# The odd mixer of a two-part block: decay as one exponential, resident gate weights, gates two projections later, 1/rms in PSUM

## The reference, cut to what matters

```python
def odd_mixer(h, w_in, conv_w, conv_b, w_rg, b_rg, w_ig, b_ig, lam, w_out):
    p = jnp.einsum("btd,dn->btn", h, w_in)
    xr, gate = jnp.split(p, [W_LRU], axis=-1)          # 1536 = 12 heads x 128 each
    xc = causal_depthwise_conv(xr, conv_w, conv_b)     # 4 taps
    xh = xc.reshape(bsz, t, LRU_HEADS, LRU_HD)
    r = sigmoid(einsum("bthi,hij->bthj", xh, w_rg) + b_rg)
    i = sigmoid(einsum("bthi,hij->bthj", xh, w_ig) + b_ig)
    log_a = -LRU_C * r * softplus(-lam)                # LRU_C = 8
    a = exp(log_a)
    mult = sqrt(-expm1(2.0 * log_a))
    bterm = mult * (i * xc)
    _, hs = associative_scan(_lin_combine, (a, bterm), axis=1)   # h = a h + b
    y = hs * silu(gate)
    return einsum("btn,nd->btd", y, w_out)
```

## Time and profile before

| | |
|---|---|
| median of 3 runs | 1165.42 us (1164.32 to 1165.55) |
| profiled execution | 1167.06 us, its span 1165.3 us |
| mean granted TensorE clock | 0.962 |
| TensorE matmul busy | 1078.4 us (93%) |
| VectorE busy | 758.8 us (65%) |
| ScalarE busy | 597.2 us (51%) |
| GpSimd busy | 600.3 us (52%) |

### The profile page before, as it was taken

The page is one execution under the profiler, slowest core; times in us unless marked ns, Lnnn a source line. Parts: engine busy times, 40 slices in busy tenths (PEclk is TensorE's granted clock), DMA queues, the critical chain, the costliest instruction groups (busy, mean ns, idle before and its releaser), DMA issues. The chain is left out here.

```text
span 1165.3 us, 21433 instructions
## 1 busy us (share of the span) xinstructions
PE 1078.4 (93%) x8189; PEld 1006.8 (86%) x8189; DVE 758.8 (65%) x1506; ACT 597.2 (51%) x1188; POOL 600.3 (52%) x453
## 2 busy tenths in 40 slices
PE   8899999999999989999999999989997879866886
PEld 8699978988889979999999999989887779655886
DVE  8859586666553245864855533369999795675964
ACT  4345667666664467644455543443334354656442
POOL 3546344445544477555344443386775654542661
PEclk9989999999999989999999999999999888888998
DMA  8224333333234423245455555544443324333342
GB/s 304 92 91 145 112 107 105 113 128 109 91 110 145 145 76 107 91 156 185 162 181 185 182 182 179 168 161 165 162 150 124 125 91 143 112 102 108 120 142 73
DMA packets 43445, 158.08 MB, mean 136 GB/s; under 512 B 4944, under 2 KB 4944, under 8 KB 43088
## 3 DMA queue, kind: packets, MB, share of 16 engines
q1 hardware_dynamic: 43200, 156.69, 39.8%
q10 hardware_dynamic: 144, 0.03, 0.0%
HBM read 155.65 MB, written 1.05 MB: 134 GB/s over the span
## 5 line engine op out<-in xcount | busy, mean ns | idle before, releaser
L1731 PE MATMUL p_proj<-arena_r,ring_hi 128*128 128x256 f32 x2208 | 661.5, 300 | 28.8 <-POOL ring_lo L548 11.1
L1732 PE MATMUL p_proj<-arena_r,ring_hi 128*128 128x256 f32 x2208 | 630.9, 286 | 0.0
L1733 PE MATMUL p_proj<-arena_r,ring_lo 128*128 128x256 f32 x2208 | 630.3, 285 | 0.0
L548 POOL TENSOR_TENSOR ring_lo<-ring,ring_hi 128x1024 fp32r<-128x1024 f32 x182 | 438.3, 2410 | 349.4 <-ACT ring_hi L877 348.5
L1731 PEld LDWEIGHTS p_proj<-arena_r,ring_hi 128*128 128x128 f32 x2208 | 429.1, 194 | 48.4 <-issue 28.3
L1732 PEld LDWEIGHTS p_proj<-arena_r,ring_hi 128*128 128x128 f32 x2208 | 430.0, 195 | 7.9 <-issue 6.0
L1733 PEld LDWEIGHTS p_proj<-arena_r,ring_lo 128*128 128x128 f32 x2208 | 429.5, 195 | 0.0
L877 ACT ACTIVATE ring_hi<-ring 128x1024 fp32r<-128x1024 f32 x276 | 290.4, 1053 | 118.8 <-PE p_proj L1733 117.8
L548 DVE TENSOR_TENSOR ring_lo<-ring,ring_hi 128x1024 fp32r<-128x1024 f32 x94 | 119.6, 1272 | 67.4 <-ACT ring_hi L877 65.9
L653 POOL TENSOR_TENSOR sbuf_s<-sbuf_s,srow 128x256 f32<-128x256 f32 (+1 forms) x48 | 41.8, 870 | 83.1 <-DVE srow L1301 58.5
L1720 PE MATMUL p_proj<-arena,ring 128*128 128x256 f32 x208 | 59.3, 436 | 24.9 <-issue 12.0
(11 more groups left out here) (274 smaller groups left out, 1243.0 us busy)
## 6 DMA issues: line engine op xcount, KB each, us to landing
ring<-w_stream SPq DMA_DIRECT2D x289, 512.0 KB, 3.3
arena<-w_tok SPq DMA_DIRECT2D x1, 1632.0 KB, 13.4
arena<-x_t SPq DMA_DIRECT2D x4, 256.0 KB, 4.9
arena<-w_cmp SPq DMA_DIRECT2D x1, 1024.0 KB, 15.3
out_t<-arena SPq DMA_DIRECT2D x4, 256.0 KB, 2.4
par<-cols SPq DMA_DIRECT2D x1, 323.0 KB, 3.0
row<-rows ACTq DMA_DIRECT2D x1, 32.0 KB, 3.2
```

The lines of the kernel that those rows point to most:

```text
L548: return eng.tensor_tensor(ring_lo[:, u % RING, :, :].rearrange("p k n -> p (k n)"), ring[:, u % RING, :, :].rearrange("p k n -> p (k n)") ...
L1731: pe.matmul(slot(s)[:, 0:S], w_hi, hi, start=(c == 0), stop=False)
L1732: pe.matmul(slot(s)[:, 0:S], w_hi, lo, start=False, stop=False)
L1733: mm = pe.matmul(slot(s)[:, 0:S], w_lo, hi, start=False, stop=(c == n - 1))
```

## The change: what it does

- xr: the conv's first part leaves ScalarE. VectorE multiplies by 1/rms, applies tap four and bias (one tensor_scalar), and adds the three taps; the banks of xr have VectorE as their only reader.
- The gates' weights (1.5 MB) are no longer in the ring. One DMA brings them into 12 free arena tiles, issued by SyncE just before the unit of even_ya[5], behind a wait for the layernorm's outputs.
- The gates of head h become one step `rgi`, two matmuls into one bank of the group `score` after xr[h+2] (heads 10 and 11: after gate[0] and gate[2]). ScalarE makes both tanh in place, U2 as before but from PSUM, and a = exp(c' r + c') into LA. The step U2 + 1 goes.
- `lru` goes: no reciprocal, no 2x - 1, no product. `lw` is two instructions: (i + 1) XC in PSUM, then (a + 1) times that into W1. `scan` multiplies W1 by U2, both in SBUF, into PSUM. The factor of `scanout` is 0.25.
- Square roots: nine heads after xr[11] (ahead of rgi of head 9), three after gate[5], each time with the table loads around them.
- scan, scanout and the split of the result run 2, 3 and 4 projections after their gate, and no longer all splits at the end.
- The copy `rin` of 1/rms in the free half of the `p_mean` bank: `hf`, `mgr` and lnv read it from there. ynorm, lnv and the last norm write it directly; for the other norms one tensor_scalar copies it at the first `hf`.

```diff
-    xr, rg_ig = jobs["xr"], jobs["rg_ig"]
     for j in range(12):
-        out.append(xr[j])
+        out.append(jobs["xr"][j])
         if j == 0:
             out += [("nsum", 3, 7), ("norm", 3)]
-        elif j not in (6, 10):
-            out.append(("scale", xr[j - 1]))
...
+        else:
+            out.append(("oconv", j - 1))
         if 2 <= j < 10:
             out += [("hf", 3, j - 2), ("split", "h3", j - 2)]
...
+        if j == 11:
+            out += [("uroot", h) for h in range(9)]
+        if j >= 2:
+            out.append(("rgi", j - 2))
+        if j >= 3:
+            out.append(("lw", j - 3))
+    gate = jobs["gate"]
     for j in range(12):
-        out.append(jobs["gate"][j])
+        out.append(gate[j])
         if j == 0:
-            out += [("uroot", h) for h in range(12)]
...
+            out += [("oconv", 11), ("lw", 9), ("gact", gate[0]), ("rgi", 10)]
+        elif j == 1:
+            out += [("lw", 10), ("gact", gate[1])]
+        else:
+            if j == 2:
+                out += [("rgi", 11)]
+            out += [("scan", j - 2), ("gact", gate[j])]
+            if j == 2:
+                out += [("lw", 11)]
+            if j == 5:
+                out += [("uroot", h) for h in range(9, 12)]
+            if j >= 3:
+                out.append(("scanout", j - 3))
+            if j >= 4:
+                out.append(("split", "ly", j - 4))
...
+                if u == first["job", "even_ya", 5] // 8:
+                    sp_eng.wait_ge(sem("yaf_ready"), 8)
+                    sp_eng.dma_start(flat(WG, 12), w_rgi).then_inc(sem("wrgi_in"), 16)
...
+                elif k == "rgi":
+                    h = s[1]
+                    ps = take(s)
+                    rg, ig = ps[:, 0:S], ps[:, S:2 * S]
+                    act.activation(rg, rg, ACT.Tanh, bias=half[:, 16 + h:17 + h], scale=0.5)
+                    act.activation(ig, ig, ACT.Tanh, bias=half[:, 28 + h:29 + h], scale=0.5)\
+                        .then_inc(sem("rgi_tanh"), 1); note(sem("rgi_tanh"))
+                    settle()
+                    act.activation(A(U2 + h), rg, ACT.Tanh, bias=half[:, 40 + h:41 + h],
+                                   scale=half[:, 40 + h:41 + h]).then_inc(sem("u_ready"), 1); note(sem("u_ready"))
+                    act.activation(A(LA + h), rg, ACT.Exp, bias=half[:, 160 + h:161 + h],
+                                   scale=half[:, 160 + h:161 + h]).then_inc(read["score", "A"], 1); note(read["score", "A"])
...
                     _, q, c = s
+                    if c == 0 and q < 4:
+                        link(dve.tensor_scalar(rin, rinv[:, :], 1.0, None, ALU.mult))
...
-                                             in1=rinv[:, :], op0=ALU.mult, op1=ALU.mult)\
+                                             in1=rin, op0=ALU.mult, op1=ALU.mult)\
...
-                        dve.tensor_tensor(A(AC + c), A(AC + c), rinv[:, :], ALU.mult).then_inc(sem("ln_z"), 1); note(sem("ln_z"))
+                        dve.tensor_tensor(A(AC + c), A(AC + c), rin, ALU.mult).then_inc(sem("ln_z"), 1); note(sem("ln_z"))
...
-                elif k == "lru":
-
-                    h = s[1]
-                    dve.wait_ge(sem("la_ready"), h + 1)
-                    link(dve.reciprocal(lru_sum(h), A(LA + h)))
-                    link(dve.tensor_scalar(A(LA + h), lru_sum(h), 2.0, -1.0, ALU.mult, ALU.add))
-                    link(dve.tensor_tensor(lru_sum(h), lru_sum(h), A(W1 + h), ALU.mult))
...
+                    was_read(dve, ("rgi", h))
+                    ig = slot(("rgi", h))[:, S:2 * S]
+                    link(dve.scalar_tensor_tensor(out=ig, in0=ig, scalar=1.0, in1=A(XC + h), op0=ALU.add, op1=ALU.mult))
+                    dve.scalar_tensor_tensor(out=A(W1 + h), in0=A(LA + h), scalar=1.0, in1=ig,
+                                             op0=ALU.add, op1=ALU.mult).then_inc(read["score", "D"], 1); note(read["score", "D"])
...
-                    link(dve.tensor_tensor(lru_sum(h), lru_sum(h), A(U2 + h), ALU.mult))
+                    link(dve.tensor_tensor(lru_sum(h), A(W1 + h), A(U2 + h), ALU.mult))
...
+                elif k == "rgi":
+                    h = s[1]
+                    readers_done(pe, s)
+                    pe.wait_ge(sem("wrgi_in"), 16)
+                    was_read(pe, ("job", "xr", h), "D")
+                    for m in range(2):
+                        mm = pe.matmul(slot(s)[:, S * m:S * m + S], wrgi[:, h, m, :], A(XC + h), start=True, stop=True)
+                    mm.then_inc(filled["score"], 1)
```

More of the change, by code:

```diff
@@ L51 @@
           ("a_gate", 8, 8), ("pool", 8, 2), ("even_yb", 8, 8), ("even_ya", 8, 8), ("xr", 12, 8), ("gate", 12, 8),
[L52 to L59, removed]
+          ("odd_out", 8, 12)]
+ON_VECTOR = {"br_dsa", "br_nsa", "br_ssd", "w_out", "ff1", "ff2", "even_yb", "even_ya", "xr", "odd_out"}
+TWICE = {"xbc", "sz", "a_gate", "b_gate", "gate"}
+LATE_TAG = {"iq": "h0u", "ik": "h0u", "dk": "h0u", "kc": "h0u", "vc": "h0u", "ks": "h0u", "kw": "h0u", "val_glu": "h2u"}
 HEAD = [("job", "iq", 0), ("job", "iq", 1), ("job", "ik", 0), ("job", "dk", 0), ("job", "kc", 0), ("job", "vc", 0),
         ("job", "ks", 0), ("job", "kw", 0)]
-LATE = HEAD + [("job", "val_glu", j) for j in range(6)] + [("job", "xr", j) for j in range(12)]
+LATE = HEAD + [("job", "val_glu", j) for j in range(6)]
 GAIN = {"h0u": "norm1", "y": "ssd_g", "h1": "norm2", "h2u": "even_g", "h3u": "odd_g"}
@@ L284, in schedule @@
+    out += [("scan", 10), ("scanout", 9), ("split", "ly", 8), ("scan", 11), ("scanout", 10), ("split", "ly", 9),
+            ("scanout", 11), ("split", "ly", 10), ("split", "ly", 11)]
     squared(4, jobs["odd_out"])
@@ L342, in psum_tenants, with program @@
     return where, turns
-def program(nc, x_t, w_stream, w_tok, w_cmp, cols, rows, out):
+def program(nc, x_t, w_stream, w_tok, w_cmp, w_rgi, cols, rows, out):
     steps = schedule()
@@ L431, in program @@
         dec = sb("dec", [P, 32])
[L432 removed]
+        half = sb("half", [P, 172])
         m8 = sb("m8", [P, 8])
@@ L479, in lru_sum @@
         def lru_sum(h):
-            at = (bank["score"] + bank["turn"] + bank["pv"])[h // 2 % 4]
+            at = (bank["turn"] + bank["pv"] + bank["score"])[h // 2 % 4]
             return at[:, S * (h % 2):S * (h % 2) + S]
@@ L749, in _ @@
             for s in steps:
-                if s in LATE:
+                if s in LATE or s[0] == "job" and s[1] == "gate":
                     continue
-                if s[0] == "scale":
+                if s[0] in ("scale", "gact"):
                     s = s[1]
@@ L1160, in _ @@
                     link(dve.tensor_scalar(half[:, 40:52], sp[:, 5, 64:76], 2.0, None, ALU.mult))
+                    link(dve.tensor_scalar(half[:, 160:172], sp[:, 5, 64:76], -4.0, None, ALU.mult))
                     dve.wait_ge(sem("ea_ready"), 1)
@@ L1450, in _ @@
                         .then_inc(sem("ybf_ready"), 1); note(sem("ybf_ready"))
-                elif k == "job" and s[1] in ON_VECTOR and s[1] != "ff1":
+                elif k == "job" and s[1] in ON_VECTOR and s[1] not in ("ff1", "xr"):
                     _, name, j = s
```

88 lines of the change are left out of this document (29 added, 59 removed).

## The result

The kernel after takes 1131.26 us in the median (1130.31 to 1133.29, 4 runs) against 1164.97 beside it: ratio 0.971, 95% interval 0.9685 to 0.9739. Forecast were 1124 and a range of 1113 to 1138. 33.7 us came instead of 41.1. The profiled execution took 1133.29 us (span 1131.5, mean clock 0.968).

The account below looks back on a forecast made before the run. Bound: TensorE's waits and low clock in the odd mixer, 50 us, from VectorE's queue. 50.0 - (3.8 + 1.4 + 0.8 + 3.4) = 40.6; less 3.0 clock, plus 3.0 and 0.5, 41.1; 1165.42 - 41.1 = 1124.3 us, range 1113 to 1138.

Parts of the forecast that it names:

- The bound: Odd mixer, square to square: 135.3 us, of which 85.3 TensorE's work and 50 waits and low clock from VectorE's queue.
- Part 1: xr turns without reciprocals: VectorE 3.9 us, TensorE 3.73; cost beyond TensorE's work 0, bounds 0 and 9 us.
- part 7: 1/rms in PSUM: 3.0 us from the layernorm's multiplications, 0.5 from hf of the even mixer and the start.
- Part 2: Gates as rgi, two projections later: 12.6 us of waits go, and the middle window's low clock with them.
- Part 3: Square roots of nine heads, then three: TensorE stalls of 3.8 us (bounds 0 and 6) and 1.4 us.
- Parts 4 and 5: Gate turns: 0.8 us lost to GpSimd, scan lock 0; end after gate[11]: 3.4 us, bounds 1 and 6.
- The clock: Remaining falls of TensorE's clock, behind the 3.8 and 3.4 us stalls: 1.4 to 2.7 us, 3.0 taken for both.
- Part 6: Gate weights in one DMA: landing 7 us after issue, cost 0; at 133 GB/s some 2 us of stall.
- The rival with the lock: Gate turns: scans wait for GpSimd, 16 us less gained, 1140; half of it, 1132. Chance 0.20, at 1134.
- The one in which all is hidden: Odd mixer: almost all waits hidden and the clock never falls, 1114 us. Chance 0.12.
- ScalarE's chain: xr turns: ScalarE's chain closes the turn, 9 us less gained, 1133. Chance 0.10.
- The rival of slower times by table loads at each head: Exp and tanh share no table, each rgi loads twice: 64 us lost against 41, about 1188. Chance 0.02.

Follow-up runs that it names:

- e6_after_recip: The kernel after with the decay by reciprocal, plain product and 2x - 1 again, its order and PSUM places kept: 1149.0 us.
- e2_rinv_sbuf: The kernel after with 1/rms back in SBUF everywhere and the copy dropped: 1146.2 us.
- e4_no_tables: The kernel after with Tanh in place of Sqrt in the root's instruction, so no change of function table in the odd mixer: 1124.0 us.
- e9_all: The kernel after with roots placed in PSUM, rgi(9) behind gate[0] and every scan one turn earlier: 1122.4 us.
- e1_scan_psum: The kernel after with the scan's product taking W1 and 1/rms in PSUM instead of W1 and the root in SBUF: 1127.6 us.
- e7_psum_root: The kernel after with the roots written or copied to PSUM by ScalarE for the scan's product, nothing left out: 1128.4 us.
- e5_before_exp: The kernel before with the decay by Exp alone, in place of reciprocal, 2x - 1 and product; old order kept: 1157.9 us.
- e11_roots84: The kernel after with PSUM roots, rgi(9) and scans moved, an early one-column tanh, and roots as eight, one xr turn earlier, then four: 1125.0 us.
- e12_scan_early: The kernel after with every scan one turn earlier and nothing else moved: 1129.3 us.
- e8_order: The kernel after with rgi(9) behind gate[0] instead of ahead of it, and every scan one turn earlier: 1125.8 us.

## Why the prediction held, and where it was short

- **The bound** (85.3 of work, 50 of waits and low clock, caused by VectorE's queue): right. e6_after_recip is the proof for the reciprocals: 2.0 us back on VectorE a head, and 15 of 30 us are gone.
- **Part 1**, xr turns at 3.9 on VectorE and 3.74 on TensorE: right to 0.01 us: VectorE's instructions repeat at 3.91 and TensorE's at 3.74. That is in part luck: oconv's tensor_scalar took 0.54 for the 0.46 put down, and the three taps 0.49 each, pipelined, for 0.51. Exp takes 0.56, between the two rows that bounded it, and no load stands between it and the tanh. But 3.9 holds only with part 7: I wrote hf at 0.51 there and sized part 7 without it. e2_rinv_sbuf shows that it is worth 10 us more there.
- **Part 2**: right; the waits of the earlier trace rows on oconv and tanh(r) are gone. Not foreseen: the table load at the first tanh and 0.6 of small pieces, 1.9 us in all.
- **Part 3**: 3.72 where I said 3.8, and 0.82 + 0.15 where I said 1.4. Right.
- **Parts 4 and 5**, the mis-sized terms. I took the lock as 0, since the scan's mean of 1.0 fitted GpSimd's 3.2, with 0.8 for the turns and 3.4 for the end. The turns did settle at 3.25, of which the lock's hold on GpSimd's split is 0.18. And VectorE had begun them late: the tanh of gate[2] stands behind rgi(11) on ScalarE, VectorE got to it at 1049.45, 3.4 us after gate[2]'s last matmul, and at 3.25 a turn against TensorE's 2.87 it never made that up. (Its 4.8 us of idle time just before are no measure of the lag: in e4_no_tables they are 2.4, and the gaps at odd_out 4.5.) What was late came due at odd_out, in gaps of 1.15, 1.70, 1.03 and 0.93 us, 4.8 in all. From 1061.85 to the square, 31.3 us hold 20.5 of work (four gates, two odd_out, one square) and 5.8 of gaps; of the 5.0 left, 1.9 stand in e9_all too, at clock 1.00: a slower pace between the gaps, whose cause is not shown. So 6.7 at the end for the 4.2 forecast. Freeing the product takes 3.6 off, in e1_scan_psum and e7_psum_root.
- **The clock**, 3.0 for both falls: it was 3.0 behind gate[2] alone (21.10 us for work of 6 x 2.87 + 0.86 = 18.1) and the other 3.1 of those 5.0 in odd_out, where the last window has 0.77. The price of one fall was right: each covered 5.5 us of work at 1.2 GHz, 25 matmuls, within the 15 to 30 and near the upper end of the 1.4 to 2.7 us read from the old chain. The step that failed is the sum: two falls make 2.8 to 5.4, and I booked 3.0.
- **Part 6**: landed 8.2 us after its issue (forecast 7); no gap at even_ya[5].
- **Part 7**: the layernorm's multiplications save 5.9 on VectorE. What of it reaches TensorE can be read from its waits between 940 and 965 us, before (first two lines) and after:

```profile
PE p_proj L1731 <- POOL arena_r L556: 3.6, 5, 1.5
PE p_proj L1731 <- DVE arena L1471: 2.9, 1, 2.9
PE p_proj L1747 <- POOL arena_r L562: 5.0, 5, 2.8
```

  The wait for VectorE is gone, but the next one, for GpSimd's split, has grown from 1.5 to 2.8. So 1.5 came where I took 3.0. The eleven traces with 1/rms in PSUM all have 4.9 to 5.0 of idle time there, the three with it in SBUF (before, e5_before_exp, e2_rinv_sbuf) 6.5 to 6.7. The `hf` of the even mixer brought more than the 0.5 put down: one gap of TensorE at 778 us went from 1.41 to 0.23, again in all eleven. Together 2.7; up to 716 us before and after are level, so the last 0.7 of the 3.4 upstream is scatter of the low clock. The sum of part 7 (3.5) was close, its two terms were not. By this trace and e2 the Trainium skill's rule ("SBUF — State Buffer", "Who interferes with whom") holds: two SBUF inputs exclude, one doesn't.

Together: 85.3 + 1.9 (xr) + 3.7 and 3.0 (roots and clock) + 1.0 (second roots) + 6.7 and 3.1 (end and clock) = 104.7 of 104.8. Against the forecast's 85.3 + 12.4 = 97.7 the seven missing are 1.9 in xr, 2.5 at the end, 3.1 of clock, less 0.5 for the roots. The median lies inside the wide range, but 1.3 above the forecast's own 1119 to 1130. That it is near the 1132 given for half the lock is chance: that sum had 8 for the lock and nothing for xr or a dearer clock. The rival with the lock named the right mechanism and was too dear: full removal of it gives 3.6, not 8 to 16. The one in which all is hidden was further off, and ScalarE's chain did not close the xr turn: TensorE had no idle moment there. The rival of slower times by table loads at each head has nothing for it. The page "ScalarE: Activation LUTs" (the Trainium skill, "Table sets: the hidden batching unit") prices a change of set at about 2.7; here it is 1.29 from the start of the load to the next instruction, at 1029.89 as at 1034.08. With that price the prediction's first stall should have read 6.6 and not 5.2, since both loads of the batch stand ahead of it; the trace has 3.7.

## What to carry to other kernels

What an edit brings depends on the others: the exponential gave 11 us in the old order with locked operands and 15 in the new one without them, and 1/rms in PSUM gave 4 and 10. When a stage's turns are about even on three engines, look at how late an engine starts the stage: here it did not catch up, and the bill came at the stage's end (two scans moved forward, into a wait, brought 2.2 us). Price an idle gap of TensorE with the clock behind it: the 3.7 us here cost 6.7. Count every fall of the clock once, and don't look at the longest gap alone: in e11_roots84 three gaps under 1.9 us had a fall behind them.

## What was not expected of the hardware

- A lock can hold its own phase. With hf in SBUF the VectorE instruction began 0.2 us behind GpSimd's in each of five turns and took 2.46 instead of 0.47, and its own delay set the next start: 2.0 us a turn for good, not the mean of a random meeting.
- The granted clock's answer to gaps on TensorE. Behind 33 us of full work, 3.72 idle was followed by 5.5 us at 1.2 GHz (after; 21 us at a mean of 0.87, as in e12_scan_early), while 2.44 and 2.15 were followed by 2.4 GHz (e8_order, e9_all). But a longest gap of 1.86, with 1.57 and 1.32 before it, was followed by 3.4 us at 1.2 GHz (e11_roots84), and the four of odd_out, none above 1.70, by 5.5 (after).
- The lock works both ways. GpSimd's 128x256 split, started while the locked product runs, takes 0.92 in the gate turns of after and 0.73 in those of e1_scan_psum, where VectorE does the same work with one SBUF input.
